# GpSimd computes the last tile's modulated expert input in place of VectorE

## What is computed

```
x  = layernorm(alpha * x + g1 * y, ln_g[0], ln_b[0])
h2 = x * (1 + sc2) + sh2                 # what the experts and the router read
scores = sigmoid(h2 @ w_router)
sel = scores + router_bias               # 4 groups of 4 experts
best group = argmax over groups of the sum of its top 2; idx = top 2 of that group
out = sum over the two experts of weight * (silu(h2 @ w1[e]) * (h2 @ w3[e])) @ w2[e]
```

## Time and profile before

| | us |
|---|---|
| runs | 2223.94, 2220.94, 2223.25 |
| median | 2223.25 |
| the profiled execution's own time | 2224.82 |
| its span, first to last instruction | 2223.0 |
| PE busy | 2111.3 (95%) |
| VectorE (DVE) busy | 1129.0 (51%) |
| ScalarE (ACT) busy | 513.0 (23%) |
| GpSimd (POOL) busy | 232.8 (10%) |

### The profile page before, as it was taken

One profiled execution on the slowest core, in us unless ns is written; L12 is line 12 of the kernel. 1 busy time (PEld: TensorE's weight loads), 2 busy tenths in 40 slices (PEclk: granted clock), 3 DMA queues, 4 the chain that ended last, 5 costly groups with the idle time before them and its releaser, 6 DMA issues. The chain is left out here.

```text
span 2223.0 us, 27264 instructions
## 1 busy us (share of the span) xinstructions
PE 2111.3 (95%) x10866; PEld 1400.2 (63%) x10866; DVE 1129.0 (51%) x1760; ACT 513.0 (23%) x997; POOL 232.8 (10%) x273
## 2 busy tenths in 40 slices
PE   7999999999999998999789999999999999979996
PEld 3457766576577644788544676656756675458883
DVE  1135458343458675664242453754434444975544
ACT  2114301242134301222130341003402441012221
POOL 1000010020100000211120002002102000011113
PEclk9999999999999999899999999999999999989998
DMA  6311166311122442799861111552111104149997
GB/s 271 135 60 38 46 216 241 114 53 61 57 60 77 168 179 114 276 365 365 270 226 41 62 39 62 208 194 84 46 61 59 32 27 185 80 175 352 362 352 200
DMA packets 67585, 334.20 MB, mean 150 GB/s; under 512 B 16968, under 2 KB 17968, under 8 KB 38336
## 3 DMA queue, kind: packets, MB, share of 16 engines
q1 hardware_dynamic: 33408, 238.70, 29.3%
q0 software_dynamic: 15040, 56.98, 8.0%
q10 hardware_dynamic: 19008, 36.74, 4.5%
HBM read 300.52 MB, written 34.49 MB: 151 GB/s over the span
## 5 line engine op out<-in xcount | busy, mean ns | idle before, releaser
L922 PE MATMUL ps<-hT,ring 128*128 128x320 f32 x2048 | 603.9, 438 | 0.0
L922 PEld LDWEIGHTS ps<-hT,ring 128*128 128x128 f32 x2048 | 369.7, 190 | 138.2 <-issue 3.3
L922 PE MATMUL ps<-ring,hT 128*128 128x512 f32 (+1 forms) x960 | 390.7, 562 | 1.2 <-ACT hT L1491 1.2
L922 PEld LDWEIGHTS ps<-ring,hT 128*128 128x128 f32 x960 | 180.5, 192 | 185.1 <-issue 177.8
L922 PEld LDWEIGHTS ps<-zT,ring 128*128 128x128 f32 x2176 | 254.8, 195 | 18.3 <-issue 15.3
L922 PE MATMUL ps<-zT,ring 128*128 128x128 f32 x2176 | 259.2, 279 | 2.2 <-ACT zT L1694 2.2
L922 PE MATMUL ps<-R,ring 128*128 128x512 f32 (+1 forms) x768 | 211.1, 435 | 4.6 <-DVE zT L2049 3.2
L1621 ACT COPY R<-ps 128x512 f32<-128x512 f32 (+2 forms) x170 | 96.0, 565 | 374.4 <-PE ps L1169 372.2
L922 PEld LDWEIGHTS ps<-R,ring 128*128 128x128 f32 x768 | 117.0, 191 | 99.3 <-issue 93.1
L922 PE MATMUL ps<-ring,zT 128*128 128x512 f32 x320 | 139.6, 594 | 0.0
L1894 DVE SCALAR_TENSOR_TENSOR R<-ring,cs,R 128x2048 f32<-128x2048 f32 x56 | 131.7, 2352 | 8.4 <-DMA ring<-in_wall 6.4
(11 more groups left out here) (290 smaller groups left out, 1935.4 us busy)
## 6 DMA issues: line engine op xcount, KB each, us to landing
ring<-in_wall SPq DMA_DIRECT2D x224, 1024.0 KB, 6.9
y_all<-R ACTq DMA_DIRECT2D x33, 512.0 KB, 10.2
R<-in_rows POOLq DMA_DIRECT2D x2, 4096.0 KB, 15.0
R<-mrows POOLq DMA_DIRECT2D x16, 512.0 KB, 18.5
R<-in_x ACTq DMA_DIRECT2D x10, 512.0 KB, 9.0
h_rows<-R ACTq DMA_DIRECT2D x10, 512.0 KB, 2.6
R<-in_bias POOLq DMA_DIRECT2D x8, 384.0 KB, 3.9
x_state<-R POOLq DMA_DIRECT2D x1, 2560.0 KB, 9.8
```

The source lines that it names most:

```text
L922: ins = nc.tensor.matmul(out, w, m, start=start, stop=stop, **kw)
```

## The change

For the context tile in each layer, the two VectorE passes are left out. GpSimd computes the same values in three passes behind the tile's power: `(x - mean) * rstd`, times `SC`, plus `SH`. The store of the context tile on ScalarE waits for the third of them, by `g_rs`, in place of `v_h2`, and GpSimd's wait for `v_h2` ahead of the second gate's rows counts one tile less. VectorE no longer waits for the h2 buffer of tile 4; GpSimd does.

```diff
                     for t in range(NT):
                         pool.wait_ge(v_lnv, (NT if layer else 0) + t + 1)
                         ch.step(nc.gpsimd.tensor_tensor(lnst[:, t, 15:16], small[:, 32 + t:33 + t], half[:, 0:1], ALU.pow), g_rs)
+                    pool.wait_ge(h_out[CTX % 2], 16 * (CTX // 2))
+                    last_h2 = h2[:, CTX % 2, :]
+                    ch.step(nc.gpsimd.tensor_scalar(last_h2, x[:, CTX, :], lnst[:, CTX, 12:13], lnst[:, CTX, 15:16], ALU.subtract, ALU.mult), g_rs)
+                    ch.step(nc.gpsimd.tensor_tensor(last_h2, last_h2, SC[:, 1, :], ALU.mult), g_rs)
+                    ch.step(nc.gpsimd.tensor_tensor(last_h2, last_h2, SH[:, 1, :], ALU.add), g_rs)
...
                         if e == 2:
-                            pool.wait_ge(v_h2, NT)
+                            pool.wait_ge(v_h2, NT - 1)
...
                     def store_h2(t):
 
-                        act.wait_ge(v_h2, t + 1)
+                        if t == CTX:
+                            act.wait_ge(g_rs, (NT if layer else 0) + NT + 3)
+                        else:
+                            act.wait_ge(v_h2, t + 1)
                         act.dma_start(A["h_rows"][128 * t:128 * t + 128, :], h2[:, t % 2, :]).then_inc(h_out[t % 2], 16)
...
                         if t == CTX:
                             latent_logits()
+                        if t == CTX:
+                            context_logits()
+                            continue
                         if t >= 2:
 
                             dve.wait_ge(h_out[t % 2], 16 * (t // 2))
                         ch.step(V_.scalar_tensor_tensor(h2[:, t % 2, :], x[:, t, :], lnst[:, t, 12:13], SC[:, v, :], ALU.subtract, ALU.mult), v_chain)
-
-                        if t == CTX:
-                            context_logits()
-                        else:
-                            dve.wait_ge(g_rs, normed + t + 1)
+                        dve.wait_ge(g_rs, normed + t + 1)
```

## The result

| | before | changed |
|---|---|---|
| median of 16 runs each, us | 2223.80 | 2227.01 |
| ratio of changed to before | | 1.0016, 95% interval 1.0009 to 1.0023 |
| profiled execution, us | 2224.82 | 2226.04 |
| span, us | 2223.0 | 2224.2 |
| GpSimd busy, us | 232.8 | 250.0 |

The change makes the kernel slower by 3.6 us (2.0 to 5.1, the ratio on 2223.8). One of the 16 runs before took 4477.75 us, twice the others, and is not in the ratio. The forecast was +6.8 us, its range -0.8 to +11.2: the sign holds and so does the kind of mechanism, the size is about half, and VectorE is held up at other steps than forecast.

What follows compares the result with a forecast made beforehand. TensorE bounds the kernel once experts run; ahead of them VectorE's chain to the index delays the first gather. Two layers by 3.4 us later gave 2223.25 + 6.8 = 2230.0 us, range 2222.5 to 2234.5.

Steps and rivals of the forecast that it cites:

- What bounds the kernel, the chain, what is removed: Ahead of each layer's experts, VectorE's chain sets the index and first gather; dropping two VectorE passes gains 1.1 us per layer.
- The term that decided, VectorE kept out: Behind tile 4's power, GpSimd passes keep VectorE's two-tensor instructions out for nearly their whole length; choice 3.4 us later per layer.
- The sizes of the passes: Three added GpSimd passes over 128x1024: 1.6 + 2.4 + 2.4 us, with gaps 6.6 together, bounds 4.0 to 8.0.
- Played through: Layer 0 walk-through: L2089 waits for pass 1, L2149 for pass 2, the next step for pass 3; 3.4 us later.
- signs of being wrong: L2149 at 880.7 beside a GpSimd pass with its usual 0.24 us, and the first gather released by the store's landing.
- The store: The context tile's h2 store on ScalarE lands at 888.8 to 889.7, hidden ahead of the index at about 891.9.
- Rival (a): VectorE not held up, the store ends the gather's wait: 0 to 0.4 us later per layer, 2223.7 us; chance 0.17.
- Rival (b): VectorE not held up, passes end by 883.4: the whole 1.1 us per layer kept, 2221.0 us; chance 0.07.
- Rival (c): GpSimd waits, the choice's dense steps keeping pass 2 out: gather 4.5 us late per layer, 2232.3 us; chance 0.08.
- The clock: TensorE's half clock around the first experts' matmuls: effect taken as none, 1.7 us per layer kept both ways.
- The forecast's numbers: Whole kernel: 2230.0 us, range 2222.5 to 2234.5; slower by over 0.2% chance 0.67, within 0.30, faster 0.03.

Runs made afterwards that it cites:

- the run without the two passes: The changed kernel without its second and third GpSimd pass (times SC, plus SH), values not right: ratio 0.9984 to the kernel before, 3.6 us below it.
- the run with one-tensor passes only: The changed kernel with its second and third GpSimd pass replaced by one-tensor passes of 1024 and 256 columns, values meaningless: ratio 1.0015 to the kernel before.
- The run with the passes alone: The kernel before with four GpSimd passes added among each layer's experts, at slots 11 to 14, results unused: one-tensor pass 4.12 us, two-tensor 2.63 us.
- both profiles with TensorE busy on the sum: The kernel before with VectorE's second tile 4 pass made by four TensorE matmuls, GpSimd given nothing, run twice: ratios 0.9983 and 0.9988.

## Why the prediction was right or wrong

**What bounds the kernel, the chain, what is removed:** right. The index ended the gather's wait before and in the change, VectorE alone gained 1.1 us (2.49 against 3.59 us for L2156), and in the run without the two passes this gain, 2.2 us in both layers, reaches the gather; the time fell by 3.6 us (1.6 to 5.6), which includes it.

**The term that decided, VectorE kept out:** right in kind. It was inferred from a power of one element that made L2119 0.03 us longer; the passes stretch single instructions by 2 us. The Trainium skill's rule of an exclusive shared port pair (SBUF — State Buffer, "SBUF: two separate sides") agrees for passes with two tensors: 2.34 us long, they let L2180 in 0.15 us before their end, so they hold nearly, not wholly, their length. It does not agree for a pass with one tensor, which let a two-tensor instruction in 1.05 us behind its start, of 3.78. There the measurement decides.

**The sizes of the passes:** the two-tensor pass was put at 2.4 and took 2.34. The one-tensor pass was put at 1.6, bounds 1.0 to 2.6, and took 3.79: the row of the memset was no floor to build on, and taking the two-tensor pass as a ceiling was wrong. One tensor with two scalars per partition costs more than two tensors.

**"Played through", the step that failed.** It had L2089 wait for pass 1, L2149 for pass 2, the next step for pass 3. L2089 and L2149 were not held up: pass 1 holds the pair only in its first us, when VectorE waits for the router. So VectorE ran the whole first part of the choice beside pass 1 and met passes 2 and 3 further down, at L2180 and L2150, with nearly their full length. Of the prediction's signs of being wrong, one half came (L2149 with its usual 0.24 us beside a pass) and the other did not (the gather was not released by the store). Counted by stalls, the prediction has three: L2089 held from 880.04 to 880.49, 0.45 us, L2149 from 881.2 to 883.1, 1.9, and the next step from 883.4 to 885.5, 2.1. That is 4.5 us less the gain of 1.1, its 3.4 per layer. Measured were two stalls, 2.03 + 1.82 = 3.85, less the same gain: 2.74, or +5.5 us in both layers in place of +6.8.

That the size came this near is in part luck. With pass 1 at its measured 3.79 us in place of 1.6, and the others at 2.34 in place of 2.4, the prediction's rule (the delay goes with the end of the passes) gives 3.4 + 2.2 - 0.1 = 5.5 us per layer, +11 in all. Two errors offset each other: the first pass was put 2.2 us too short, and it was wrongly taken to hold VectorE to its end.

**The store:** right that it stays hidden; it was to land 2 to 3 us ahead of the index and landed 1.0 ahead, for the slow first pass. Rival (a) is a real second arm, seen in the run with one-tensor passes only. Its price was put a little low: with the gather 0.83 us behind the landing, as in that run, landings of 888.5 to 889.4 give a gather at 889.3 to 890.2, not 889.8 at most. Rival (b), the passes done by 883.4, was out of reach: the three take 8.6 us. Rival (c) is refuted by the rows of passes 2 and 3, which start 0.08 to 0.09 us behind the pass ahead.

**The clock:** taken as nothing, with 1.7 us per layer either way. The gather's shifts give +5.5 us, the two comparisons 3.6 and 4.4. Windows over the experts' first matmuls as far as the half clock (1.2 GHz) lasts, before and in the change (columns as in the earlier trace rows):

```profile
896.95:900.36 3.41, 3.41 (x16) 3.41 (x17) 3.00 (x13) 0.00 (x0) 0.00 (x0) 0.50 0.87 294
1983.51:1989.21 5.70, 5.70 (x26) 5.70 (x27) 5.18 (x16) 0.00 (x0) 0.00 (x0) 0.50 0.57 193
```

```profile
898.65:901.80 3.15, 3.15 (x14) 3.15 (x15) 2.78 (x11) 0.00 (x0) 0.00 (x0) 0.50 0.82 262
...
1987.78:1990.65 2.87, 2.86 (x13) 2.87 (x14) 2.49 (x12) 0.00 (x0) 0.00 (x0) 0.50 0.88 342
```

9.1 us against 6.0 here; in the second profiles 11.5 (5.32 + 6.14) against 9.1 (5.69 + 3.40). Half of the difference is what it is worth at full clock: 1.4 us given back on the mean of two pairs, about what is missing. But one stretch varies by 2 to 3 us from execution to execution of the same code: 3.41 and 5.32 in layer 0 of the kernel before, 3.15 and 5.69 in the change. The run with the passes alone, which adds nothing between the power and slot 11 of either layer, had 5.56 + 3.11 = 8.7, less than the second profile of the change. So this is where the sizes point and not shown. It stays open.

**The forecast's numbers:** the time, 2227.0, lies in the range of 2222.5 to 2234.5. By the ratio it is 0.16% slower, which by the bound of 0.2% counts as no change, given 0.30, though the interval lies clear of 1; slower by more had 0.67. The chance of a time below 2.2 us per layer (short passes, or the clock giving back) was set at 0.12 within the forecast, and 1.8 per layer is what the ratio gives. The gather's delay was 2.74, so without the part that is open above it would not have come to this; the stall at L2089 that did not happen had no chance of its own.

## What to carry to other kernels

A GpSimd pass off the critical path is not free where VectorE is on it: count each large GpSimd pass with two tensors that overlaps a chain of small VectorE steps with two SBUF tensors as one stall of nearly its length (1.7 to 2.2 us for 2.34 here), whether or not anyone waits for its result. A pass with one tensor cost VectorE only what fell into its first 1.05 us, except for a converting copy. Before work is moved, ask which engine neither is on the chain nor shares with it; here that was TensorE, mostly idle for 14 us, where an add with a scale per partition is two matmuls, with an identity and a diagonal, for each 512 columns. And when a store is moved with its producer, compare its landing with the other arm: it was hidden here only because the index had become late.

## What the hardware showed that was not expected

- A GpSimd pass over 128x1024 float32 with one tensor and two scalars per partition takes 3.79 us, one with two tensors 2.34 us.
- The first kind keeps VectorE's two-tensor instructions out for about its first 1.05 us only, the second kind until 0.15 to 0.21 us before its end.
- VectorE's reductions of one tensor (L2177, L2181) ran at their usual 0.24 and 0.29 us beside two-tensor passes, but a converting copy (L2187, 0.20 us) beside a one-tensor pass took 0.88 and ended 0.06 us behind it.
- In both profiles with TensorE busy on the sum, the half clock came 7.6 to 10.3 us behind the power in place of 1.6 to 4.8 in all others, and lasted 13.65 us in place of 17.07 to 27.31. Layer 0 of the first, 8.4 us behind:

```profile
885.61:899.26 13.65, 7.00 (x42) 6.36 (x43) 10.94 (x43) 1.01 (x1) 4.36 (x5) 0.50 0.59 195
```
